# Two convolution tiles as matmuls over four taps on shifted copies, in the mixers of a two-block model

## The chip, the core and the metric

One core of a Trainium2 chip runs the whole program. Its engines work in parallel, each through its own list of instructions in order: TensorE (PE; matmuls, with weight loads as PEld), VectorE (DVE), ScalarE (ACT), GpSimd (POOL) and SyncE (SP), which here only issues transfers (DMA). Engines wait for each other by semaphores. The metric is the device time of one execution in microseconds; lower is better.

## What is computed

Batch 1, 256 positions, width 1024, float32. A first block of two layers (a gated memory cell beside retention) is followed by a second block of two layers; each of these is a mixer and a feed-forward part, dense in the first layer and a mixture of experts in the second. The change is in the mixer:

```python
def conformer_conv(u, conv_w, conv_b, ln_g, ln_b):
    a, g = jnp.split(u, 2, axis=-1)
    z = a * jax.nn.sigmoid(g)
    z = lax.conv_general_dilated(z, conv_w, window_strides=(1,),
        padding=[(CONV_WIDTH - 1, 0)], feature_group_count=D_CONV, ...) + conv_b
    z = layernorm(z, ln_g, ln_b)
    return jax.nn.silu(z)

# in each layer of the second block
proj = h @ w_in[l]
y_conv = conformer_conv(u_conv, ...)
y_att = chunk_band_attention(q, k, v, ...)      # 8 heads of 64
x = x + g1 * (jnp.concatenate([y_conv, y_att], axis=-1) @ w_out[l])
```

The convolution is depthwise and causal: 512 channels, 31 taps each, and its layer norm runs over the 512 channels.

## The kernel before

Everything lies transposed, channels on the 128 partitions and the 256 positions along the rows, so 512 channels are four tiles of 128 x 256.

**Units.** All weights go by in units of 1 MB (128 x 2048). For each unit SP loads it into a slot of `raw` (`load`), ScalarE rounds it to the matmul's type (`high`, line 730, `whi`), VectorE computes the remainder (`low`, line 1757, `wlo`), and TensorE makes three products for each tile pair (high by high, high by low, low by high). `whi` and `wlo` have three slots each: `high` of unit n waits until TensorE is done with unit n - 3 (`unit_done`). `low` hands the raw slot back to SP (`raw_free`). This order is written out by hand in each engine's part; there is no scheduler.

**A mixer** has 10 units of `w_in` (`MIX_COLS` gives the 256-column group of each) and 4 units of `w_out`. Of the 10 units two give the gate (`MIX_SIG`), two the value that it is multiplied with (`MIX_Z`), two the attention's values (`MIX_V`), and four q and k (`MIX_QK`). The functions are `mixer` in the parts of ScalarE, TensorE and VectorE, and `mixer_loads` in SP's.

- ScalarE computes the gate (`sigmoid`), takes q, k and values out of PSUM, the softmax's exponentials (`weights`, `scaled`), the turned weights (`take_turned`), and at the end squares, root and silu of the convolution's norm.
- VectorE computes z = (1 + gate) x value for two tiles at a time into `zpad`, which has 30 zeros ahead of the 256 positions. Then it goes through the taps of tiles 0 and 1, one instruction of 128 x 256 for each tap and tile (62), and after them those of tile 2 (31, in two sums, and an addition: lines 2135 and 2139). The taps are spread between the lows and the attention's steps (`conv(n)`).
- Tile 3 is TensorE's: `diag` holds for each tap a 32 x 32 diagonal of weights in each of the four groups of 32 partitions, and `conv` (line 1478) multiplies it with a shifted view of `zpad`. That is 31 taps x 4 groups = 124 products of 32 x 32 x 256, in three blocks between the attention's last steps. ScalarE takes the result (line 1019).
- `diagonals()` on VectorE builds `diag` once a mixer, with one product of 992 elements (line 2157).
- After the last attention step TensorE runs output unit 0 (`out_unit(0)`: attention's tiles, ready first), the mean over the four convolution tiles (line 1548), three adaptation rows (`ada_rows`, line 1469, products of 128 x 32 x 256 over four groups of columns), the variance (line 1555, over the squares that ScalarE made, line 1024), and output units 1 to 3.

ScalarE's order at this end matters below:

```python
act.wait_ge(tile_done, l + 1)
nc.scalar.activation(zacc[:, CT - 1], ps2[bank_g][:, 0], ACT.Identity, bias=...)
high(Unit(first + 13))
for p in range(2):
    act.wait_ge(zc_ready, 2 * l + p + 1)
    nc.scalar.activation(sq2[:, 0, 2 * p:2 * p + 2], zacc[:, 2 * p:2 * p + 2], ACT.Square)
```

`high` of unit first + 13 waits for unit first + 10, which is output unit 0.

Of the kernel before, what the change touches and what calls it, by code (L numbers as in the profile page):

```python
# [5 lines left out]
F32 = mybir.dt.float32  # L6
# [6 lines left out]
P = 128  # L13
S = 256
# [71 lines left out]
CONV_STEPS = 3 * CW + 1  # L86
# [173 lines left out]
def two_block_model(nc, x, positions, consts, c, w_ada, b_ada, norm_g, w_in, conv_w, conv_b, b_igate, b_fgate,  # L260
# [7 lines left out]
    with ctx:  # L268
# [3 lines left out]
        def sem(name):  # L272
# [95 lines left out]
        zpad = sb("zpad", [P, CT, CW - 1 + S], F32, b2)  # L368
# [14 lines left out]
        b2.close()  # L383

# [46 lines left out]
        diag = cst[:, C_CAUSAL:C_CAUSAL + CW * GROUP].rearrange("p (a m) -> p a m", a=CW)  # L431
# [51 lines left out]
        diag_ready, tile_done, tile_taken = sem("diag_ready"), sem("tile_done"), sem("tile_taken")  # L483
# [11 lines left out]
        logits_done, e_ready, route_ready, rank_done, jobs_ready, htok_done, htok_ready = (  # L495
            sem("logits_done"), sem("e_ready"), sem("route_ready"), sem("rank_done"), sem("jobs_ready"),
# [14 lines left out]
        def _(sp):  # L511
# [54 lines left out]

            def mixer_loads(l, first):
# [155 lines left out]
        def _(act):  # L723
# [186 lines left out]
            def mixer(l, first):  # L910
# [82 lines left out]
                take_values(1)  # L993
# [6 lines left out]
                sigmoid(1)  # L1000
# [18 lines left out]
                nc.scalar.activation(zacc[:, CT - 1], ps2[bank_g][:, 0], ACT.Identity, bias=par2[:, l, P2_CB + CT - 1:P2_CB + CT])\  # L1019
                    .then_inc(tile_taken, 1)  # L1020
# [45 lines left out]
            act.wait_ge(e_ready, 1)  # L1066
# [61 lines left out]
        def _(pe):  # L1128
# [289 lines left out]
            def mixer(l, first):  # L1418
# [55 lines left out]
                def conv(of):  # L1474

                    for tap in of:
                        for g in range(0, P, GROUP):
                            last = mm(ps2[bank_g][g:g + GROUP, 0], diag[g:g + GROUP, tap], zpad[g:g + GROUP, CT - 1, tap:tap + S],  # L1478
                                      start=tap == 0, stop=tap == CW - 1)
                    if of[-1] == CW - 1:  # L1480
                        last.then_inc(tile_done, 1)
# [5 lines left out]
                if l:  # L1487
# [3 lines left out]
                        8: (qk_taken, 4 * l + 4), 9: (v2_ready, 2 * l + 2)}  # L1491
# [1047 lines left out]
```

## Time and profile before

| | |
|---|---|
| three timed runs | 2111.48, 2113.81, 2115.74 us, median 2113.81 |
| profiled execution, first to last instruction (span) | 2109.6 us |
| TensorE busy | 2063.4 us (98% of the span) |
| VectorE busy | 1759.2 us (83%) |
| ScalarE busy | 1321.1 us (63%) |
| TensorE's granted clock | 0.993 of full speed over the span, 1.00 in both mixers |
| first mixer | about 643 to 762 us of the span |
| second mixer | about 972 to 1090 us |

The profiled execution has no time of its own beside its span; what lies around the span is in the timed runs only. TensorE's busy time comes from matmuls whose ends are modelled, and they overlap in the pipeline, so the idle time between them is the better sign. A printed wait in a timeline stands in brackets behind the row, with what ended it.

### The profile page before, as it was taken

Reading aid. Unit: us, or ns where it says so; the run is one execution under the profiler, and the core shown is the slowest. Engines: PE = TensorE matmul, PEld = TensorE weight load, DVE = VectorE, ACT = ScalarE, POOL = GpSimd, SP = SyncE. Lnnn points to the kernel's source line nnn. Section 1 sums busy time; section 2 is a strip of 40 time slices with the busy share of each in tenths; the row PEclk is TensorE's granted clock in tenths of the full one; section 3 lists DMA queues with packets and bytes.
Section 4 is the critical chain, followed back from the end, with each engine's and each line's share of the span. In section 5 each row is a group of like instructions: output and inputs, shape, how many; then the busy total and the mean of one; then the engine's idle time right before and its main releaser. Section 6 shows DMA issues by size and latency. Waiting matters only on the chain.

```text
span 2109.6 us, 33770 instructions
## 1 busy us (share of the span) xinstructions
PE 2063.4 (98%) x13553; PEld 1837.5 (87%) x13553; DVE 1759.2 (83%) x2177; ACT 1321.1 (63%) x1265; POOL 30.5 (1%) x60
## 2 busy tenths in 40 slices
PE   7999999999999999999989999999999999999998
PEld 5999999999999889999878888888888888888887
DVE  3898976888759888888878888888888888888887
ACT  3655645566645663435757777776777776776775
POOL 3000000000000000000000000000000000000000
PEclk8999999999999999999999999999999999999999
DMA  9788855776656379986448999999999999999995
GB/s 297 248 261 249 250 199 160 220 220 204 216 184 220 117 225 308 317 308 220 141 163 306 361 355 348 379 348 347 357 356 376 349 345 356 365 365 344 360 344 195
DMA packets 356160, 595.05 MB, mean 282 GB/s; under 512 B 10376, under 2 KB 201368, under 8 KB 356008
## 3 DMA queue, kind: packets, MB, share of 16 engines
q1 hardware_dynamic: 352864, 586.92, 80.7%
q0 software_dynamic: 2752, 5.86, 1.1%
q8 instruction: 109, 1.79, 0.4%
q14 instruction: 43, 0.35, 0.0%
q10 hardware_dynamic: 392, 0.13, 0.0%
HBM read 591.80 MB, written 4.22 MB: 283 GB/s over the span
## 4 chain that ended last, share of the span: by engine, by line
PE 84%; DVE 9%; ACT 3%; issue 2%; DMA 1%; POOL 0%; SPq 0%; DVEq 0%; POOLq 0%
PE ps L1660 9%; PE ps L1662 9%; PE ps L1661 9%; PE ps L1150 6%; PE ps L1152 5%; PE ps L1151 5%; PE ps L1691 5%; PE ps L1690 5%; PE ps L1689 5%; PE ps L1205 3%; PE ps L1207 3%; PE ps L1206 3%; DVE wlo L1757 3%; PE ps L1635 1%; PE ps L1478 1%
## 5 line engine op out<-in xcount | busy, mean ns | idle before, releaser
L1757 DVE TENSOR_TENSOR wlo<-raw,whi 128x2048 fp32r<-128x2048 f32 x485 | 1108.9, 2288 | 206.9 <-ACT whi L730 206.5
L730 ACT CAST whi<-raw 128x2048 fp32r<-128x2048 f32 x485 | 926.6, 1911 | 376.2 <-PE ps L1662 133.2
L1150 PE MATMUL ps<-hhi,whi 128*128 128x256 f32 x1360 | 387.4, 285 | 0.5 <-DVE wlo L1757 0.5
L1152 PE MATMUL ps<-hhi,wlo 128*128 128x256 f32 x1360 | 379.8, 279 | 0.0
L1151 PE MATMUL ps<-hlo,whi 128*128 128x256 f32 x1360 | 379.5, 279 | 0.0
L1660 PE MATMUL ps<-whi,xghi 128*128 128x512 f32 x896 | 360.3, 402 | 0.7 <-DVE wlo L1757 0.7
L1662 PE MATMUL ps<-wlo,xghi 128*128 128x512 f32 x896 | 350.2, 391 | 0.0
L1661 PE MATMUL ps<-whi,xglo 128*128 128x512 f32 x896 | 348.9, 389 | 0.0
L1150 PEld LDWEIGHTS ps<-hhi,whi 128*128 128x128 f32 x1360 | 255.8, 188 | 7.6 <-issue 7.3
L1151 PEld LDWEIGHTS ps<-hlo,whi 128*128 128x128 f32 x1360 | 255.9, 188 | 0.3
L1152 PEld LDWEIGHTS ps<-hhi,wlo 128*128 128x128 f32 x1360 | 255.6, 188 | 0.0
L1662 PEld LDWEIGHTS ps<-wlo,xghi 128*128 128x128 f32 x896 | 168.1, 188 | 36.6
L1660 PEld LDWEIGHTS ps<-whi,xghi 128*128 128x128 f32 x896 | 168.3, 188 | 33.9 <-DVE wlo L1757 1.2
L1661 PEld LDWEIGHTS ps<-whi,xglo 128*128 128x128 f32 x896 | 168.6, 188 | 33.6
L1689 PE MATMUL ps<-whi,thi 128*128 128x512 f32 x448 | 175.2, 391 | 0.0
L1691 PE MATMUL ps<-wlo,thi 128*128 128x512 f32 x448 | 174.8, 390 | 0.0
L1690 PE MATMUL ps<-whi,tlo 128*128 128x512 f32 x448 | 174.6, 390 | 0.0
L1813 DVE SCALAR_TENSOR_TENSOR acc<-raw,cact,acc 128x256 f32<-128x256 f32 x324 | 132.8, 478 | 0.0
L1691 PEld LDWEIGHTS ps<-wlo,thi 128*128 128x128 f32 x448 | 84.1, 188 | 17.8
L1690 PEld LDWEIGHTS ps<-whi,tlo 128*128 128x128 f32 x448 | 84.1, 188 | 16.9
L1689 PEld LDWEIGHTS ps<-whi,thi 128*128 128x128 f32 x448 | 84.1, 188 | 16.8
L1191 PE MATMUL ps<-whi,hhi 128*128 128x256 f32 x320 | 91.8, 287 | 0.0
(400 smaller groups left out, 2991.4 us busy)
## 6 DMA issues: line engine op xcount, KB each, us to landing
raw<-in_moe_w_gate_dram SPq DMA_DIRECT2D x112, 1024.0 KB, 5.9
raw<-in_moe_w_up_dram SPq DMA_DIRECT2D x112, 1024.0 KB, 5.8
raw<-in_moe_w_down_dram SPq DMA_DIRECT2D x112, 1024.0 KB, 5.2
raw<-in_w_in_dram SPq DMA_DIRECT2D x92, 1024.0 KB, 5.5
raw<-in_w_ada_dram SPq DMA_DIRECT2D x69, 1024.0 KB, 7.9
raw<-in_w_out_dram SPq DMA_DIRECT2D x24, 1024.0 KB, 5.2
raw<-in_ffn_w_gate_dram SPq DMA_DIRECT2D x11, 1024.0 KB, 9.2
raw<-in_ffn_w_up_dram SPq DMA_DIRECT2D x11, 1024.0 KB, 9.1
```

Source lines behind the costliest of these rows:

```text
L730: nc.scalar.copy(whi[:, u.hl, :], raw[:, u.raw, :]).then_inc(hi_ready, 1)
L1150: mm(ps2[u.bank][:, j], whi[:, u.hl, w], hhi[:, k], start=k == 0, stop=False)
L1151: mm(ps2[u.bank][:, j], whi[:, u.hl, w], hlo[:, k], start=False, stop=False)
L1152: last = mm(ps2[u.bank][:, j], wlo[:, u.hl, w], hhi[:, k], start=False, stop=k == KD - 1)
L1660: mm(o, xghi[:, k, x], whi[:, u.hl, w], start=k == 0, stop=False)
L1661: mm(o, xglo[:, k, x], whi[:, u.hl, w], start=False, stop=False)
L1662: last = mm(o, xghi[:, k, x], wlo[:, u.hl, w], start=False, stop=k == KD - 1)
L1689: mm(o, thi[:, f], whi[:, u.hl, w], start=f == 0, stop=False)
L1690: mm(o, tlo[:, f], whi[:, u.hl, w], start=False, stop=False)
L1691: last = mm(o, thi[:, f], wlo[:, u.hl, w], start=False, stop=f == FE // P - 1)
L1757: V.tensor_tensor(wlo[:, u.hl, :], raw[:, u.raw, :], whi[:, u.hl, :].bitcast(F32), ALU.subtract).then_inc(raw_free, 1)
L1813: last = V.scalar_tensor_tensor(sums[k % 2], w[:, k], cact[:, block, k:k + 1], sums[k % 2], ALU.mult, ALU.add)
```

## The change

In each of the two mixers:

- Tiles 2 and 3 are both TensorE's. For each tile t and each group g of 32 channels, SP makes four copies of the group's rows of `zpad`, each one position further on, and stacks them on the 128 partitions. A product with such a stack (128 rows) and a matrix of 128 x 32 that holds four diagonals sums four taps. 31 taps are 8 steps (`TAP_STEPS`), each reading the stack four positions further. 2 tiles x 8 steps x 4 groups = 64 products of 128 x 32 x 256.
- The copies are `shifts(l)`, 20 transfers from SP: 12 of 32 x 2 x 284 elements (both tiles) and 8 of 32 x 284. They go into `h`, which is free then, and the last stack into `acc`. SP issues them behind the load of unit first + 12 and waits for z of tiles 2 and 3 first. Loads of later units stand behind them.
- VectorE's `diagonals()` builds two matrices of 128 x 1024 in place of one of 128 x 992, from 16 small copies of taps. They lie in the parts of `y2hi` and `y2lo` that are written later. VectorE keeps the taps of tiles 0 and 1 only.
- The gate's second unit comes one place forward (units 7 and 8 give z of tiles 2 and 3, unit 9 the second half of the values), `z(1)` stands right behind the low part of unit 9, `sigmoid(1)` takes the place of `take_values(1)` on ScalarE, and that stands later.
- On TensorE adaptation rows and mean stand ahead of output unit 0; the variance stands behind it.
- In the expert layer the semaphore `e_ready` is merged into `route_ready`.

The diff, cut to its core:

```diff
-MIX_COLS = (2, 0, 4, 6, 8, 5, 7, 9, 3, 1)
-MIX_SIG, MIX_Z, MIX_V, MIX_QK = (0, 8), (1, 9), (4, 7), (2, 3, 5, 6)
+MIX_COLS = (2, 0, 4, 6, 8, 5, 7, 3, 1, 9)
+MIX_SIG, MIX_Z, MIX_V, MIX_QK = (0, 7), (1, 8), (4, 9), (2, 3, 5, 6)
...
+            def shifts(l):
+                sp.wait_ge(z_ready, 2 * l + 2)
+                for g in range(P // GROUP):
+                    for o in range(TAPS_AT_ONCE):
+                        to, of = slice(GROUP * o, GROUP * o + GROUP), zpad[GROUP * g:GROUP * g + GROUP, 2:4, o:o + ZW]
+                        if g < 3:
+                            sp.dma_start(zflat[to, 2 * ZW * g:2 * ZW * g + 2 * ZW].rearrange("p (t x) -> p t x", t=2), of).then_inc(shifted_in, 16)
+                        else:
+                            for t in range(2):
+                                sp.dma_start(shifted(t, g)[to], of[:, t]).then_inc(shifted_in, 16)
...
                     load(Unit(first + MIX_UNITS + j), ...)
+                    if j == 2:
+                        shifts(l)
...
# ScalarE
-                take_values(1)
+                sigmoid(1)
                 pair_high(0)
...
-                sigmoid(1)
                 pair_high(1)
...
                     take_turned(n)
+                take_values(1)
                 for n in (6, 7):
                     weights(n)
...
-                act.wait_ge(tile_done, l + 1)
-                nc.scalar.activation(zacc[:, CT - 1], ps2[bank_g][:, 0], ...)
+                for t in range(2):
+                    act.wait_ge(tile_done, 2 * l + t + 1)
+                    nc.scalar.activation(zacc[:, 2 + t], ps2[bank_g][:, t], ...)
                 high(Unit(first + 13))
...
# TensorE
+                def conv(t, of):
+                    for m in of:
+                        for g in range(P // GROUP):
+                            at = GROUP * (TAP_STEPS * g + m)
+                            last = mm(ps2[bank_g][GROUP * g:GROUP * g + GROUP, t], sdiag[t][:, at:at + GROUP],
+                                      shifted(t, g)[:, TAPS_AT_ONCE * m:TAPS_AT_ONCE * m + S], start=m == 0, stop=m == TAP_STEPS - 1)
...
-                pe.wait_ge(sig_ready, 2 * l + 2)
                 pe.wait_ge(z_ready, 2 * l + 2)
-                conv(range(0, 10))
+                pe.wait_ge(shifted_in, 16 * SHIFTS * (l + 1))
+                conv(0, range(TAP_STEPS))
+                pe.wait_ge(v2_ready, 2 * l + 2)
                 weighted(4)
                 weighted(5)
-                conv(range(10, 18))
+                conv(1, range(4))
                 turn_weights(6)
                 turn_weights(7)
-                conv(range(18, CW))
+                conv(1, range(4, TAP_STEPS))
                 weighted(6)
                 weighted(7)
-                out_unit(0)
+                for i in range(rows - HALF, rows):
+                    ada_rows(i)
+                pe.wait_ge(conv_step, CONV_STEPS * (l + 1))
                 for t in range(CT):
...
                     last = mm(ps2[bank_a][:, 0], mean512[:], zacc[:, t], start=t == 0, stop=t == CT - 1)
                 last.then_inc(zmean_done, 1)
-                for i in range(rows - HALF, rows):
-                    ada_rows(i)
+                out_unit(0)
...
# VectorE
-                    V.tensor_tensor(diag, sel.unsqueeze(1).broadcast_to([P, CW, GROUP]), ...)
+                    of = taps2[:, l].rearrange("p (m o t) -> p o t m", o=TAPS_AT_ONCE, t=CT)
+                    for o in range(TAPS_AT_ONCE):
+                        for g in range(P // GROUP):
+                            last = V.tensor_copy(wst[GROUP * o:GROUP * o + GROUP, :, g], of[GROUP * g:GROUP * g + GROUP, o, 2:4])
+                    step(last)
+                    for t in range(2):
+                        last = V.tensor_tensor(sdiag[t][:]..., sel..., wst[:, t]..., ALU.mult)
...
                 low(Unit(first + 9))
+                z(1)
...
                 low(Unit(first + 10))
-                z(1)
...
-                conv(4)
+                conv(len(taps))
                 pair_low(2)
-                conv(len(taps) - 8)
                 pair_low(3)
-                conv(len(taps))
                 dve.wait_ge(zmean_done, l + 1)
```

How instructions stand on the engines, at three places of the first mixer.

TensorE, its end, before: the last products of output unit 0 (line 1205 and on), mean (`mean512` with `zacc`), adaptation rows (`cpad`), variance (`mean512` with `h`), and output unit 1.

```order
L1205 MATMUL ps5<-y2hi,whi 128x256
L1206 MATMUL ps5<-y2lo,whi 128x256
L1207 MATMUL ps5<-y2hi,wlo 128x256
L1548 MATMUL ps1<-zacc,mean512 128x256 x4
L1469 MATMUL ps7<-raw,cpad 32x256 x24
L1555 MATMUL ps0<-h,mean512 128x256 x4
L1205 MATMUL ps2<-y2hi,whi 128x256
```

The same end now, from the last weighted sums (`pT,v2`) to the start of output unit 0:

```order
L1488 MATMUL ps6<-pT,v2 64x256
L1489 MATMUL ps6<-pT,v2 64x128
L1499 MATMUL ps7<-raw,cpad 32x256 x24
L1580 MATMUL ps1<-zacc,mean512 128x256 x4
L1235 MATMUL ps2<-y2hi,whi 128x256
```

and from the end of output unit 0 on:

```order
L1235 MATMUL ps5<-y2hi,whi 128x256
L1236 MATMUL ps5<-y2lo,whi 128x256
L1237 MATMUL ps5<-y2hi,wlo 128x256
L1586 MATMUL ps0<-h,mean512 128x256 x4
L1235 MATMUL ps2<-y2hi,whi 128x256
```

Mean and adaptation rows went ahead of output unit 0, and nothing stands between it and the variance any more. On ScalarE the order there is the one before: take the tiles, high part of unit 13, squares.

SP, its transfers at the end of the first mixer, before: the four loads of output units stand in a row, behind the last ones of `w_in`.

```order
L520 DMA raw<-in_w_in_2_dram 128x8x256
L533 DMA raw<-in_w_ada_2_dram 128x8x256
L520 DMA raw<-in_w_out_2_dram 128x2x1024 x4
L520 DMA raw<-in_ffn_w_gate_2_dram 128x8x256
L533 DMA raw<-in_w_ada_2_dram 128x8x256
```

Now:

```order
L535 DMA raw<-in_w_out_2_dram 128x2x1024 x3
L589 DMA h<-zpad 32x2x284 x12
L592 DMA h<-zpad 32x284
L592 DMA acc<-zpad 32x284
L592 DMA h<-zpad 32x284
L592 DMA acc<-zpad 32x284
L592 DMA h<-zpad 32x284
L592 DMA acc<-zpad 32x284
L592 DMA h<-zpad 32x284
L592 DMA acc<-zpad 32x284
L535 DMA raw<-in_w_out_2_dram 128x2x1024
```

The 20 copies stand ahead of the load of the last output unit.

VectorE, the preparation of the diagonals behind the first z, before:

```order
L2117 SCALAR_TENSOR_TENSOR zpad<-sig,ps1 128x2x256
L2151 MEMSET cst 64x64
L2152 MEMSET cst 64x64
L2155 MEMSET cst 64x64 x2
L2156 TENSOR_REDUCE cst<-cst 128x32
L2157 TENSOR_TENSOR cst<-cst,taps2 128x992
L1757 TENSOR_TENSOR wlo<-raw,whi 128x2048
```

Now:

```order
L2149 SCALAR_TENSOR_TENSOR zpad<-sig,ps1 128x2x256
L2178 MEMSET cst 64x64
L2179 MEMSET cst 64x64
L2182 MEMSET cst 64x64 x2
L2183 TENSOR_REDUCE cst<-cst 128x32
L2187 COPY cst<-taps2 32x2x8 x16
L2190 TENSOR_TENSOR sdiag0<-cst 128x1024
L2190 TENSOR_TENSOR sdiag1<-cst 128x1024
L1788 TENSOR_TENSOR wlo<-raw,whi 128x2048
```

The low part of unit 4 stands behind 16 copies and two products where it stood behind one product.

## Rows read from the trace of the kernel before

**Rows 1.** Table of stretches, first mixer: busy us (instructions) by engine, clock, DMA share, GB/s
```profile
core 0: us, PE busy (x) PEld busy (x) DVE busy (x) ACT busy (x) POOL busy (x), PEclk, DMA share, GB/s
640.00:770.00 130.00, 125.65 (x1190) 110.36 (x1189) 109.13 (x226) 83.53 (x140) 0.91 (x1) 1.00 0.55 179
```

**Rows 2.** Timeline of TensorE, first mixer: start us, length us, engine, line, operation, count
```profile
715.46 4.52 PE L1478 MATMUL ps<-zpad,cst 32*32 32x256 f32 x80 [0.36 <-DVE zpad L2117]
...
720.72 3.66 PE L1478 MATMUL ps<-zpad,cst 32*32 32x256 f32 x64
...
725.12 5.82 PE L1478 MATMUL ps<-zpad,cst 32*32 32x256 f32 x104
...
731.67 0.39 PE L1205 MATMUL ps<-y2hi,whi 128*128 128x256 f32 x1
...
737.52 1.89 PE L1548 MATMUL ps<-zacc,mean 128*128 128x256 f32 x8
739.34 2.80 PE L1469 MATMUL ps<-raw,cpad 128*32 128x256 f32 x48
742.07 1.99 PE L1555 MATMUL ps<-h,mean 128*128 128x256 f32 x8
```

**Rows 3.** Timelines of VectorE (first row) and ScalarE, end of the first mixer
```profile
735.85 0.42 DVE L2139 TENSOR_TENSOR zacc<-zacc,sig 128x256 f32<-128x256 f32 x1
...
737.78 1.90 ACT L730 CAST whi<-raw 128x2048 fp32r<-128x2048 f32 x1 [5.21 <-PE ps L1207]
740.17 1.23 ACT L1024 ACTIVATE h<-zacc 128x512 f32<-128x512 f32 x2 [0.49 <-DVE zacc L2253]
```

**Rows 4.** Timeline of VectorE, first mixer: low part of unit 9, second z
```profile
705.30 2.28 DVE L1757 TENSOR_TENSOR wlo<-raw,whi 128x2048 fp32r<-128x2048 f32 x1
...
714.63 0.68 DVE L2117 SCALAR_TENSOR_TENSOR zpad<-sig,ps 128x512 f32<-128x512 f32 x1
```

**Rows 5.** Transfers: issues by SP and ScalarE (timelines), median us to landing, landings in mixer
```profile
0.72 0.77 SPq L513 DMA_DIRECT2D crow<-in_c_dram  x2
1.54 0.36 SPq L514 DMA_DIRECT2D cst<-in_consts_dram  x1
...
1.40 0.28 ACTq L788 DMA_DIRECT2D prow<-in_norm_g_dram  x1
...
2103.01 1.84 SPq L620 DMA_DIRECT2D out_dram<-h  x4
...
707.62 0.37 SPq L520 DMA_DIRECT2D raw<-in_w_out_dram  x1
...
out_dram<-h SPq DMA_DIRECT2D x4, 256.0 KB, 2.9
...
cst<-in_consts_dram SPq DMA_DIRECT2D x1, 64.0 KB, 1.9
...
DMA to landing us min/median/max: 4.8/8.0/13.3
```

**Rows 6.** Timelines of VectorE and TensorE, first mixer: diagonals, small operations, heads, scores
```profile
661.30 1.19 DVE L2157 TENSOR_TENSOR cst<-cst,taps 128x992 f32<-128x992 f32 x1
...
754.78 0.23 DVE L2271 TENSOR_TENSOR mod<-ps,par 128x6 f32<-128x6 f32 x2
...
651.78 0.18 DVE L2190 COPY cpad<-cact 128x8 f32<-128x8 f32 x1
...
680.62 1.41 DVE L2146 SCALAR_TENSOR_TENSOR q<-q,par,rs 128x512 f32<-128x512 f32 x2
...
682.11 0.50 PE L1440 MATMUL ps<-q 64*128 64x128 f32 x4
```

**Rows 7.** Timelines of VectorE and TensorE, second mixer: waits, heads, scores
```profile
994.68 2.29 DVE L1757 TENSOR_TENSOR wlo<-raw,whi 128x2048 fp32r<-128x2048 f32 x1 [0.60 <-ACT whi L730]
...
1007.20 0.75 DVE L2146 SCALAR_TENSOR_TENSOR q<-q,par,rs 128x512 f32<-128x512 f32 x1 [0.37 <-ACT rs L942]
...
1009.34 0.50 PE L1440 MATMUL ps<-q 64*128 64x128 f32 x4
...
1016.56 1.24 PE L1449 MATMUL ps<-cst,p 128*128 128x128 f32 x6 [0.50 <-ACT p L957]
```

More of the change, by code:

```diff
@@ L367, in two_block_model @@
         y2lo = sb("y2lo", [P, KD, S], F32R, b2)
-        zpad = sb("zpad", [P, CT, CW - 1 + S], F32, b2)
+        zpad = sb("zpad", [P, CT, CW + S], F32, b2)
         zacc = sb("zacc", [P, CT, S], F32, b2)
@@ L383, in two_block_model, with shifted @@
         b2.close()
+        bd = ExitStack()
+        sdiag = [sb("sdiag0", [P, TAP_STEPS * P], F32, bd)]
+        sb("between_sdiag", [P, (KD - CT) * S], F32, bd)
+        sdiag.append(sb("sdiag1", [P, TAP_STEPS * P], F32, bd))
+        bd.close()
+        zflat = h[:].rearrange("p k s -> p (k s)")
+        zspare = acc[:, 0:2].rearrange("p k s -> p (k s)")
+        def shifted(t, g):
+            return zspare[:, 0:ZW] if (t, g) == (1, P // GROUP - 1) else zflat[:, ZW * (2 * g + t):ZW * (2 * g + t) + ZW]
         bf = ExitStack()
@@ L1472, in ada_rows @@
                     last.then_inc(ada_done, 1)
[L1474 to L1480, printed above, removed]
+                def conv(t, of):
[4 more added lines that the diff above has]
+                                      shifted(t, g)[:, TAPS_AT_ONCE * m:TAPS_AT_ONCE * m + S], start=m == 0, stop=m == TAP_STEPS - 1)
+                    if of[-1] == TAP_STEPS - 1:
                         last.then_inc(tile_done, 1)
@@ L2108, in mixer @@
                 n0, bank_a = NH2 * l, Unit(first + 9).bank
-                taps = [(t, tap) for tap in range(CW) for t in range(2)] + [(2, tap) for tap in range(CW)]
+                taps = [(t, tap) for tap in range(CW) for t in range(2)]
                 done = CONV_STEPS * l
@@ L2116, in z @@
                     dve.wait_ge(unit_done, u.done())
-                    V.scalar_tensor_tensor(zpad[:, 2 * i:2 * i + 2, CW - 1:], sig[:], 1.0, ps2[u.bank], ALU.add, ALU.mult)\
+                    V.scalar_tensor_tensor(zpad[:, 2 * i:2 * i + 2, CW - 1:CW - 1 + S], sig[:], 1.0, ps2[u.bank], ALU.add, ALU.mult)\
                         .then_inc(z_ready, 1)
@@ L2124, in conv @@
                         t, tap = taps.pop(0)
-                        at = done + 3 * CW - len(taps)
-                        to = sig[:, 1] if t == 2 and tap % 2 else zacc[:, t]
+                        at = done + CONV_STEPS - len(taps)
+                        to = zacc[:, t]
                         w, src = taps2[:, l, tap * CT + t:tap * CT + t + 1], zpad[:, t, tap:tap + S]
@@ L2130, in conv @@
                             last = V.tensor_scalar(to, src, w, par2[:, l, P2_CB + t:P2_CB + t + 1], ALU.mult, ALU.add)
-                        elif t == 2 and tap == 1:
-                            last = V.tensor_scalar(to, src, w, None, ALU.mult)
                         else:
@@ L2136, in conv @@
                         last.then_inc(conv_step, 1)
-                        if not taps:
-                            dve.wait_ge(conv_step, at)
-                            V.tensor_tensor(zacc[:, 2], zacc[:, 2], sig[:, 1], ALU.add).then_inc(conv_step, 1)
                 def norm_heads(half):
@@ L2186, in mixer @@
                 V.memset(zpad[:, :, 0:CW - 1], 0.0)
+                V.memset(zpad[:, :, CW - 1 + S:], 0.0)
                 V.memset(mean512[:], 1.0 / D_CONV)
```

39 lines of the change are left out of this document (22 added, 17 removed).

## The prediction

> **What bounds the kernel now.** I read the table of stretches first: in the first mixer's stretch TensorE is busy 125.65 of 130 us, VectorE 109.13 [rows 1]. So TensorE is the engine to shorten, and a microsecond counts where TensorE works less or waits less. Next the timeline of the first mixer's second half [rows 2]. The reader is to see a TensorE that hardly stops: the three convolution blocks start at 715.46, 720.72 and 725.12, output unit 0 at 731.67, the mean at 737.52, the adaptation rows at 739.34, the variance at 742.07, each about where the one before it ends. The only printed wait is 0.36 before the convolution. The second mixer runs the same code. Busy times of adjacent groups overlap by some hundredths, so sums below are good to about 0.1 a term.
>
> **Convolution on TensorE.** Now 124 products of form 32x32 take 4.52 + 3.66 + 5.82 = 14.00 us [rows 2]. (The counts there are twice as large, since weight loads are counted too.) Afterwards there are 2 tiles x 8 steps x 4 groups = 64 products of form 128x32. That form is in the trace: 24 adaptation products, also over four column groups, take 2.80, 0.117 each [rows 2]. 64 x 0.117 = 7.5. **-6.5 per mixer.** I see no reason for much less or more: same form, same columns, same type.
>
> **VectorE loses its third tile**, 31 taps and an addition. That work is not on the path: its last addition runs from 735.85 to 736.27 [rows 3], and the mean follows output unit 0 at 737.52 [rows 2] without a wait. Removed it gives **0** by itself; it only lets the mean stand ahead of output unit 0.
>
> **The shifted copies, a new wait.** The convolution now needs 20 transfers, which SP issues after z of the second pair. z moves right behind the low part of unit 9, which ends at 705.30 + 2.28 = 707.58, and takes 0.68 [rows 4]: done at 708.2. SP issued the load that stands ahead, unit 12's, at 707.62 for 0.37 [rows 5], so it is free. What do 20 issues cost? Two issues at the program's start span 0.72 to 1.54, 0.41 each [rows 5]. The twentieth starts at 708.2 + 19 x 0.41 = 716.0. How long a small transfer takes from issue to landing has two near rows: 1.9 (64 KB into SBUF) and 2.9 (256 KB to DRAM) [rows 5]. A copy has 71 KB, so I take 2.0: all landed at 718.0. The convolution started at 715.46. **+2.5 per mixer**, the printed wait of 0.36 included. Behind this wait on TensorE stand weighted sums 4 to 7 and everything after them; nothing can step in. Bounds: the quickest issue of a small load is 0.28 [rows 5], 0.31 apart, and 1.9 to land gives 716.0 (+0.5); four stores in 1.84, 0.46 apart [rows 5], and 2.9 to land give 719.8 (+4.3).
> SP's next load, unit 13's, slips by two microseconds from 714.7 and is not needed before output unit 0 is over. ScalarE's second sigmoid changes places with taking the values; its table load falls into ScalarE's wait for unit 7, and what is left (some tenths later for weights 4 and 5) lies under the wait for the copies.
>
> **Squares behind a cast, a second new wait.** On ScalarE the order at the end is unchanged: take the tiles, high part of unit 13, squares. The high part waits until output unit 0 is done: it ran at 737.78, 0.26 after the mean's start, for 1.90, and the squares followed at 740.17 [rows 3]. Today TensorE has the mean (1.89) and the adaptation rows (2.80) in that time and arrives at the variance at 742.07 [rows 2], after the squares. In the change the mean and the rows stand ahead of output unit 0, and the variance directly behind it. So after output unit 0 TensorE waits for 0.26 + 1.90 and the first square, half of 1.23: 0.26 + 1.90 + 0.62 = 2.8. **+2.75 per mixer**; I see no smaller end than 2.4, as ScalarE's order is fixed, and none above 3.2. What follows the variance (root, scaling, silu) follows it as before, under output unit 1.
>
> **VectorE's preparation.** It gets 16 copies of 16 elements and two products of 1024 elements in place of one of 992. Two small operations take 0.23 together, 0.15 for the second and so 0.08 from start to start [rows 6]: 15 x 0.08 + 0.15 = 1.4. The product of 992 takes 1.19 [rows 6], one of 1024 so 1.23, and 1.2 is added. Sum +2.6. If each copy costs what the 128x8 copy takes alone, 0.18 [rows 6], it is 2.9 + 1.2 = +4.1; I take the nearer row, two in succession.
> Who pays? In the first mixer's timeline VectorE has no wait from 661.30 until it has normalized the heads, 680.62 to 682.03, and TensorE's first scores stand at 682.11 [rows 6], 0.08 later. (Lows and taps fill the time between.) So the delay reaches TensorE: **+2.5 in the first mixer**. In the second, VectorE waits 0.60 and then 0.37, its normalized heads are ready at 1007.95 for scores at 1009.34, 1.4 later, and TensorE waits 0.50 at 1016.56 for ScalarE [rows 7]. Together 2.9. That takes up the delay: **+0.1 in the second**.
> The Trainium skill speaks against many small operations here. Its page VectorE: DVE Perf Modes, section The TRN2 errata, gives a fixed cost for each instruction, 58 cycles by its table and about 150 by its measurement of single operations, at 0.96 GHz. By 150 the 16 copies would take an estimated 2.8 us instead of 1.4, and the sum would be 1.4 higher; by 58 they take 1.2, which agrees with the row of two in succession, 0.08 apart.
>
> **The sum.** First mixer: -6.5 + 2.5 + 2.75 + 2.5 = +1.25. Second: -6.5 + 2.5 + 2.75 + 0.1 = -1.15. Together +0.1. The profiled execution has a span of 2109.6; the median of the runs, 2113.81, lies 4.2 above it, and I add the same: 2109.7 + 4.2 = 2113.9. A measurement of this kernel can tell about 0.2%, 4.2 us, from no change: the bounds are 2109.6 and 2118.0.
>
> **Rivals.**
> Slower: the copies queue behind the load issued 0.6 earlier. Loads of a megabyte in this stretch, some of them issued right behind another, took 4.8 to 13.3 to land [rows 5]; the 20 copies are another megabyte behind unit 12's. Should they be done 13.3 after 708.2, at 721.5, each mixer loses 3.5 more: 2113.9 + 7.0 = 2120.9. It turns out slower by over 0.2% once the copies land more than 2.1 later than 718.0 in both mixers. For it: each copy touches 32 partitions at a time, which no row shows. Against it: the transfer engines are busy 0.55 of this stretch [rows 1], and 20 issues spread the copies over 8 us. Costly copies on VectorE (+1.5, first mixer) push the same way.
> By the Trainium skill, page SBUF — State Buffer, section Door 1, a transfer over 32 partitions reaches 8 of 16 ports, 27.2 GB/s each. By that a copy's 73 KB need an estimated 0.33 us, less than an issue; only together with the load ahead would it end past the last issue, by some tenths. No row here has such a transfer.
> Faster: issue and landing go at their quick ends, 2.0 less per mixer, 2109.9; if VectorE's delay in the first mixer is taken up as well (2.5), 2107.4. Against the latter speaks the 0.08 above.
> The change doesn't do what it says: the 128x32 products do not overlap over column groups. A full product takes 1.89 / 4 = 0.47 [rows 2]; 64 of them cost 30 instead of 7.5, +45 for both mixers, 2159. The adaptation rows at 0.117 speak against it.
>
> **How the numbers follow.** Forecast 0.62; slower rival with costly copies 0.24; faster rival 0.13; no overlap 0.01. The forecast and the quick end at 2109.9 lie within 0.2%, but part of the faster rival's chance lies past 2109.6. Faster 0.12, same 0.63, slower 0.25. The bounds of the issues (-4.0, +3.6) and of the copies (+1.5) span 2109.9 to 2119.0; with a part of both rivals the range is 2108 to 2120.
>
> **What would show it.** In the trace of the changed kernel: 64 convolution products in 7.5 us a mixer; TensorE waiting some 2.5 (2 to 3) for a transfer of zpad before the first of them; a second wait of 2.75 before the variance, behind ScalarE's cast; a stall of 2.5 spread over unit 4 and the first scores in the first mixer only; the third tile's taps gone from VectorE without effect. The prediction is wrong if the copies land before TensorE gets there, if the squares are ready at the end of output unit 0, or if unit 4 and the scores start on time.

## The result, and the profile after

The changed kernel takes 2132.86 us (median of 4 runs, 2132.27 to 2133.36); the kernel before took 2114.05 in the same rounds. The ratio is 1.009, with a 95% interval of 1.0078 to 1.0103: **slower by 18.8 us**. The forecast was 2113.9 with a range up to 2120. It was wrong. Its chance for this side, 0.25, stood mainly on copies that queue behind a load, which did not happen, and for a small part on costly copies on VectorE, which did. The profiled executions have spans of 2109.6 before and 2131.5 after, 21.9 apart; the accounts below are made against these 21.9. The profiled execution after is that of the slowest run (2133.36), 0.5 above the median. Besides, a run's time exceeds its span by 1.9 in the changed kernel and by 2.3 to 3.0 in the kernel before, in the rounds of the experiments; the forecast had added 4.2. The rest of the 3.1 us by which 21.9 exceeds 18.8 is less than the spread of the kernel before, 4.3.

Lines of the changed kernel lie 27 to 35 further down: the convolution is L1509, the variance L1586, the output units L1235 to L1237, the cast L759, the low part L1788, the copies' issues L589 and L592.

First the page of the kernel after: TensorE is at 97% of a longer span.

```profile
span 2131.5 us, 33306 instructions
...
PE 2062.4 (97%) x13313; PEld 1836.9 (86%) x13313; DVE 1741.7 (82%) x2151; ACT 1321.8 (62%) x1267; POOL 30.6 (1%) x60
```

Next the waits of TensorE: us in total, times, longest. Before, the convolution waited twice for z (0.36 in the first mixer [rows 2]), 0.7 in all, and no counterpart of the other three was over 0.5.

```profile
PE ps L1509 <- DMA acc<-zpad: 14.6, 2, 7.4
...
PE ps L1586 <- ACT h L1054: 5.1, 2, 2.6
...
PE ps L1221 <- DVE wlo L1788: 3.2, 3, 2.7
...
PE ps L1470 <- DVE q L2173: 1.3, 1, 1.3
```

The first is the wait for the copies, twice 7.3. The second is the wait for the squares, twice 2.57. The last two stand behind the preparation on VectorE: unit 4 in the first mixer (2.7) and the first scores in the second (1.3). Together 24 us, where the forecast had 5.0 + 5.5 + 2.6 = 13.

Then the timeline of TensorE. The first three rows are the first mixer, the last two the second mixer's first scores and convolution; in brackets the wait just before.

```profile
668.65 0.36 PE L1221 MATMUL ps<-whi,hhi 128*128 128x256 f32 x1 [2.73 <-DVE wlo L1788]
...
726.63 5.78 PE L1509 MATMUL ps<-h,sdiag 128*32 128x256 f32 x64 [7.11 <-DMA acc<-zpad]
...
751.54 3.62 PE L1586 MATMUL ps<-h,mean 128*128 128x256 f32 x8 [2.57 <-ACT h L1054]
...
1023.12 0.50 PE L1470 MATMUL ps<-q 64*128 64x128 f32 x4 [1.30 <-DVE q L2173]
...
1064.26 5.93 PE L1509 MATMUL ps<-h,sdiag 128*32 128x256 f32 x64 [7.45 <-DMA acc<-zpad]
```

Two things are to be seen. The waits for the copies are near 7, not 2.5. And what comes right behind a wait is slow: the variance's products take 3.62, where before they took 1.99 [rows 2]; the first 32 convolution products (counted as 64 with their loads) take 5.78, where 3.66 is their time at full speed, as an experiment below shows; and some 16 products of unit 4 start 0.21 apart where 0.12 is usual, 1.6 us in all. The table of stretches says why (busy us by engine, TensorE's clock as a share of full speed, share of the transfer engines, GB/s):

```profile
core 0: us, PE busy (x) PEld busy (x) DVE busy (x) ACT busy (x) POOL busy (x), PEclk, DMA share, GB/s
668.70:672.70 4.00, 4.00 (x22) 4.00 (x23) 4.00 (x12) 0.29 (x1) 0.00 (x0) 0.60 0.76 251
...
719.00:726.00 7.00, 0.53 (x6) 0.12 (x3) 6.04 (x20) 4.02 (x14) 0.00 (x0) 0.87 0.33 79
726.00:733.00 7.00, 6.37 (x72) 3.48 (x72) 0.00 (x0) 0.00 (x0) 0.00 (x0) 0.64 0.45 155
733.00:740.00 7.00, 7.00 (x111) 3.96 (x110) 0.85 (x2) 4.15 (x7) 0.00 (x0) 1.00 0.00 0
...
751.50:754.50 3.00, 2.96 (x7) 2.43 (x8) 0.00 (x0) 2.04 (x3) 0.00 (x0) 0.50 1.03 325
...
778.00:781.00 3.00, 3.00 (x19) 3.00 (x19) 3.00 (x9) 3.00 (x8) 0.00 (x0) 0.63 0.01 3
...
1064.00:1068.00 4.00, 3.75 (x36) 2.02 (x40) 0.00 (x0) 0.00 (x0) 0.00 (x0) 0.50 0.76 266
```

While TensorE waits, or within a microsecond of its new start (unit 4), its clock falls from 2.4 to 1.2 GHz (a share of 0.50), and it stays there for some microseconds of work. Before, the first mixer stood at 1.00 throughout [rows 1]. The page TensorE: Matmul & The Clock Gate of the Trainium skill, section HAM oscillation — how this bites in real kernels, describes this: a wait for a transfer between blocks of products puts the clock down, and the block behind the wait starts at the low level. The trace agrees, and the prediction had no term for it. Not every wait has this behind it: the start of the dense layer waits 2.17 in both kernels, and the products behind it ran at 1.00 before and at 0.63 after (778 to 781). Which short waits put the clock down stays open.

SP's timeline tells where the 7 us come from (SPq is SP issuing a transfer).

```profile
711.94 8.16 SPq L589 DMA_DIRECT2D h<-zpad  x12
720.15 0.59 SPq L592 DMA_DIRECT2D h<-zpad  x1
...
724.64 0.59 SPq L592 DMA_DIRECT2D acc<-zpad  x1
```

Twenty issues take 13.3 us, from 711.94 to 725.23. Transfers of zpad land 1.9 to 5.3 after their issue, 2.2 in the median; TensorE starts at 726.63, 2.0 after the last issue began. So the last copy arrives as fast as forecast, but the copies are sent 0.63 to 0.68 apart instead of 0.41.

VectorE's preparation, and ScalarE at the end of the first mixer:

```profile
661.04 2.87 DVE L2187 COPY cst<-taps 32x16 f32<-32x16 f32 x16
663.94 2.36 DVE L2190 TENSOR_TENSOR sdiag<-cst 128x1024 f32<-128x1024 f32 x2
```

```profile
749.06 1.90 ACT L759 CAST whi<-raw 128x2048 fp32r<-128x2048 f32 x1 [9.29 <-PE ps L1237]
750.86 1.14 ACT L1054 ACTIVATE h<-zacc 128x512 f32<-128x512 f32 x2
```

**Account of the 21.9 us.** The changed kernel comes to the first mixer 0.3 earlier than the kernel before. In the first mixer: unit 4 and what follows it +4.1, for VectorE is that late (it begins to normalize the heads at 684.43, before at 680.62 [rows 6], and the 0.3 comes on top); TensorE spends it as a wait of 2.73 and as low clock behind it. Weights 4 and 5 +0.6, since ScalarE does its second sigmoid ahead of them; the wait for the copies +6.75 (7.11 less the 0.36 of before); the convolution -6.5 in products, +2.1 for the low clock; the wait for the squares +2.57, and +1.6 for the variance at the low clock. Sum +11.2; the timelines say that the mixer takes 11.4 longer. Second mixer: +1.0 preparation (the wait of 1.30, less some tenths taken back behind it), +0.6, +7.1 (7.45 less the 0.31 of before), -6.5 + 2.3, +2.57, +1.6, sum +8.7; the timelines say +8.9. The start of the dense layer behind the first mixer costs 1.2 more, by the clock of 0.63 shown above; the start of the expert layer behind the second costs 0.5 more, by a wait of 3.64 instead of 3.15. 11.4 + 8.9 + 1.2 + 0.5 - 0.3 = 21.7. These are readings; the experiments test the parts.

### The profile page after: what moved, and what is told of

Its sections match the earlier page's. It is cut to its first block, busy times and chain, and to the rows that moved or that the text cites. A ratio compares the mean times of both kernels' runs of the same rounds, so it can differ in the third digit from the quotient of the medians.

```text
span 2131.5 us, 33306 instructions
## 1 busy us (share of the span) xinstructions
PE 2062.4 (97%) x13313; PEld 1836.9 (86%) x13313; DVE 1741.7 (82%) x2151; ACT 1321.8 (62%) x1267; POOL 30.6 (1%) x60
## 4 chain that ended last, share of the span: by engine, by line
PE 82%; DVE 9%; ACT 3%; issue 3%; DMA 2%; SPq 1%; DVEq 0%; ACTq 0%
PE ps L1693 9%; PE ps L1691 9%; PE ps L1692 9%; PE ps L1180 5%; PE ps L1181 5%; PE ps L1182 5%; PE ps L1722 5%; PE ps L1721 5%; PE ps L1720 5%; PE ps L1235 3%; PE ps L1236 3%; PE ps L1237 3%; DVE wlo L1788 3%; PE ps L1666 1%; ACT whi L759 1%
## 5 line engine op out<-in xcount | busy, mean ns | idle before, releaser
L1788 DVE TENSOR_TENSOR wlo<-raw,whi 128x2048 fp32r<-128x2048 f32 x485 | 1108.8, 2288 | 205.7 <-ACT whi L759 205.3
L759 ACT CAST whi<-raw 128x2048 fp32r<-128x2048 f32 x485 | 926.6, 1911 | 384.1 <-PE ps L1693 133.6
```

The lines of the kernel that those rows point to most:

```text
L759: nc.scalar.copy(whi[:, u.hl, :], raw[:, u.raw, :]).then_inc(hi_ready, 1)
L1788: V.tensor_tensor(wlo[:, u.hl, :], raw[:, u.raw, :], whi[:, u.hl, :].bitcast(F32), ALU.subtract).then_inc(raw_free, 1)
```

## Experiments

The theory after the result (A in the expectations): the loss has four parts, the copies' issues on SP, the clock that falls in the waits, the preparation on VectorE, and the squares behind the cast. The main rivals: the transfers themselves are slow or disturb other traffic, and the issue is dearer because of where its data comes from.

Times "below the change" are differences of medians from different rounds; in them the kernel before had 2114.05 (the change), 2113.81 (experiments 1 to 4) and 2112.84 (6 and 7). With the intervals of the ratios a difference of 5 can be 2 or 8, so where two accounts lie closer the rows decide and not the time.

**1. The copies left out.** The change without its 20 transfers and without the wait for them; its convolution of tiles 2 and 3 reads whatever lies in the buffers, so it is a measurement and not a kernel to use.

```diff
-                    if j == 2:
-                        shifts(l)
...
-                pe.wait_ge(shifted_in, 16 * SHIFTS * (l + 1))
```

> The changed kernel without its 20 copies a mixer and without TensorE's wait for them (part left out: the convolution of tiles 2 and 3 reads whatever lies in the buffers). Theory A (the loss is mostly the wait for the copies, 7.1 and 7.45 us, and the clock that it halves, 5.78 instead of 3.64 us for the first 32 products, twice): 14.6 + 4.3 = 18.9 us less than the changed kernel, 2114. Rival B (the 128x32 products are slow by themselves after the attention's products): the wait goes but the first block stays at 5.8 us, 2118. Rival C (the wait only takes the place of another, on ScalarE or VectorE): above 2124.

Measured: 2112.7 us, ratio 0.9995 (0.9985 to 1.0004). The copies and what hangs on them cost 20.2 us: 14.6 of waiting, 4.4 of low clock in the convolution by the timelines, and 1.2 that this run does not assign. Its first 32 products run at full clock:

```profile
719.76 3.66 PE L1507 MATMUL ps<-h,sdiag 128*32 128x256 f32 x64
```

What follows is sobering: even if the copies were free, the change would only break even. It saves 13 us of products, and the two other waits, with their clock, take these back.

**2. Squares ahead of the cast.** One line of ScalarE's order moved.

```diff
-                high(Unit(first + 13))
                 for p in range(2):
                     act.wait_ge(zc_ready, 2 * l + p + 1)
                     nc.scalar.activation(sq2[:, 0, 2 * p:2 * p + 2], zacc[:, 2 * p:2 * p + 2], ACT.Square).then_inc(zsq_ready, 1)
+                high(Unit(first + 13))
```

> The changed kernel with ScalarE's two squares ahead of the high part of unit 13. Theory A (TensorE's 2.57 us before the variance is ScalarE's order, and the variance's slow 3.6 instead of 2.0 us is the clock that this wait halves): 2 x (2.57 + 1.6) = 8.3 us less, 2124.5. Rival B (the clock is halved by the earlier, longer wait anyway): 5.1 us less, 2127.7. Rival C (something else, such as VectorE's subtraction, is late by as much): under 2 us less.

Measured: 2124.85, ratio 1.0055 (1.0038 to 1.0072), 8.0 below the change, as expected. By the time alone that is not clear of the 5.1 of the two waits; the row is, for the variance is back at full clock and directly behind output unit 0. (A new wait of 0.9 a mixer, for VectorE's low part ahead of output unit 1, takes a part back.)

```profile
748.52 1.89 PE L1586 MATMUL ps<-h,mean 128*128 128x256 f32 x8
```

**3. TensorE kept busy while it waits.** 58 products whose results are not used stand ahead of the wait for the copies; the copies are untouched.

```diff
+                for _ in range(58):
+                    mm(ps2[bank_g][:, 0], hhi[:, 0, 0:P], hhi[:, 0], start=True, stop=True)
                 pe.wait_ge(shifted_in, 16 * SHIFTS * (l + 1))
```

> The changed kernel with 58 products without use (128x256, 0.117 us each, 6.8 us) between the last scores and the wait for the copies; nothing waits for them. Theory A (the first block takes 5.8 us because the granted clock is halved after 7 us without work): the clock stays at 1.00, the block takes 3.7, 2 x 2.1 = 4.2 us less than the changed kernel, 2128.7. Rival B (the block's length is the products' own, or bank or operand effects): no gain, and if the products overrun the wait, a loss of up to 1 us.

Measured: 2128.37, ratio 1.0065 (1.0048 to 1.0082), 4.5 below the change. The convolution starts as long behind the first copy's issue as in the change (14.7), and its first 32 products take 3.66 instead of 5.78, in the second mixer too:

```profile
726.06 3.66 PE L1509 MATMUL ps<-h,sdiag 128*32 128x256 f32 x64
```

So the second part of the loss at the copies is the clock, not the form of the products.

**4. The copies in the kernel before, with nobody on TensorE waiting.** In the first mixer they come from zpad, in the second the same shapes come from a weight in DRAM.

```diff
+                        to, of = slice(GROUP * o, GROUP * o + GROUP), zpad[GROUP * g:GROUP * g + GROUP, 2:4, o:o + 283]
+                        if l:
+                            of = w_in_2[1].rearrange("(k p) n -> p k n", p=P)[GROUP * g:GROUP * g + GROUP, 2:4, o:o + 283]
...
+                    if j == 2:
+                        shifts(l)
```

> The kernel before with 20 such copies a mixer added behind the load of unit 12; in the first mixer from zpad, in the second of the same shape from a weight in DRAM. TensorE waits for none (the squares at the end do, long after). Theory A (an issue of such a copy holds SP for 0.59 us and more wherever it comes from, since 20 stand in a row; the copies themselves disturb nobody): issues 0.63 apart in both mixers, time within 0.1% of the kernel before. Rival B (the source in SBUF makes the issue dear): 0.63 in the first mixer, 0.41 in the second. Rival C (traffic of the copies slows loads): over 2 us slower than before.

Measured: 2114.17, ratio 1.0001 (0.9991 to 1.0011). The traffic costs nothing that shows (the interval is 2 us either way), so it is the waiting for it that costs. SP's timeline, first mixer and then the second:

```profile
715.32 8.31 SPq L577 DMA_DIRECT2D h<-zpad  x12
723.68 0.59 SPq L579 DMA_DIRECT2D h<-zpad  x1
...
1044.46 6.73 SPq L577 DMA_DIRECT2D h<-in_w_in_dram  x12
1051.23 0.42 SPq L579 DMA_DIRECT2D h<-in_w_in_dram  x1
1051.70 0.42 SPq L580 DMA_DIRECT2D acc<-in_w_in_dram  x1
```

The same shape costs SP 0.59 from zpad and 0.42 from DRAM. The rows by line add that the first twelve are no dearer each; a few long ones lift their mean (ns, shortest / median / longest):

```profile
L577 SPq DMA_DIRECT2D h<-zpad x12: 594/597/1120, 715.3 to 723.0; - x12
L577 SPq DMA_DIRECT2D h<-in_w_in_dram x12: 343/427/1647, 1044.5 to 1050.8; - x12
```

**5. Source, place, rows or bytes?** Two looks, both again with transfers that no product waits for. First, from zpad, 20 transfers of one row of 100 numbers, over 32 partitions in the first mixer and over 128 in the second:

```diff
+                for i in range(20):
+                    if l:
+                        sp.dma_start(zflat[:, 100 * i:100 * i + 100], zpad[:, 2 + i % 2, i // 2:i // 2 + 100]).then_inc(shifted_in, 16)
+                    else:
+                        part = slice(GROUP * (i % 4), GROUP * (i % 4) + GROUP)
+                        sp.dma_start(zflat[part, 100 * i:100 * i + 100], zpad[0:GROUP, 2 + i % 2, i // 2:i // 2 + 100]).then_inc(shifted_in, 16)
```

> The kernel before with 20 transfers from zpad in SBUF issued by SP where the change issues its copies; nobody on TensorE waits for them. First mixer: 20 transfers of 32 partitions with one row of 100 numbers (12.5 KB); second mixer: 20 transfers of 128 partitions with one row of 100 numbers (50 KB). Theory A (the source decides what an issue costs): both series are 0.6 to 0.65 us apart, as the transfers of zpad of 32 partitions with 283 numbers were (0.635), whatever the bytes. Rival B (the number of rows decides, for a given source): the series of 128 partitions is clearly dearer, at or above the 0.69 of the transfers with 64 rows, and the series of 32 partitions stays at 0.635. Rival C (the bytes decide): the series of 12.5 KB falls below 0.5. The time stays within 0.2% of the kernel before in each case.

Second, from DRAM, the change's shapes in the first mixer and 128 partitions in the second:

```diff
+                        to, of = slice(GROUP * o, GROUP * o + GROUP), rows_in[GROUP * g:GROUP * g + GROUP, 2:4, o:o + 283]
...
+                        sp.dma_start(zflat[:, 100 * i:100 * i + 100], rows_in[:, 2 + i % 2, i // 2:i // 2 + 100]).then_inc(shifted_in, 16)
```

> The kernel before with 20 transfers from DRAM issued by SP where the change issues its copies; nobody on TensorE waits for them. First mixer: the 20 transfers in the shape of the change (32 partitions, two rows of 283 numbers, the last eight with one row), from a weight in DRAM. Second mixer: 20 transfers of 128 partitions with one row of 100 numbers from the same weight. It answers whether the cheaper issue from DRAM came from the source or from the place: that run had SBUF as the source in the first mixer and DRAM in the second. Theory A (the source): the first mixer's last eight are 0.47 apart, as they were in the second. Rival D (the place): they are 0.635 apart. For the series of 128 partitions theory A expects about 0.47, rival B (rows decide) 0.56 or more. The time stays within 0.2% of the kernel before in each case.

One time each, 2114.7 and 2113.53 beside 2112.41 of the kernel before. SP's rows by line, of the run from zpad (32 partitions, then 128):

```profile
L576 SPq DMA_DIRECT2D h<-zpad x20: 577/591/1484, 714.7 to 728.5; - x20
...
L573 SPq DMA_DIRECT2D h<-zpad x20: 533/602/1823, 1044.1 to 1057.9; - x20
```

and of the run from DRAM (the change's shapes, then 128 partitions):

```profile
L578 SPq DMA_DIRECT2D h<-in_w_in_dram x12: 348/427/1602, 714.8 to 721.1; - x12
...
L584 SPq DMA_DIRECT2D h<-in_w_in_dram x20: 340/432/1212, 1043.7 to 1053.4; - x20
```

The median is 0.59 to 0.60 from zpad and 0.42 to 0.43 from DRAM, whatever the place, the partitions (32 or 128) or the bytes (12.5 to 71 KB). Theory A, the source, holds for the median; rivals B, C and D fall. The means came out dearer than I expected, though: 0.73 apart from zpad instead of 0.60 to 0.65, and 0.51 instead of 0.47 from DRAM, by single issues of 1.2 to 1.8 us. What makes those is open. So is whether the source alone decides: the four stores from h to DRAM, also from SBUF, are 0.46 apart [rows 5].

**6. The preparation moved.** The 16 copies and two products no longer stand with the diagonals but some steps later, behind conv(4) and conv(6), where VectorE has slack.

```diff
                 conv(4)
+                prep_copies()
                 pair_low(0)
                 conv(6)
+                prep_products()
                 norm_heads(1)
```

> The changed kernel with VectorE's 16 small copies and two products moved from ahead of unit 4's low part to places where VectorE waits later (copies ahead of the low part of heads 0 and 1, products ahead of the second normalization of heads). Theory A (their 5.2 us instead of 1.2 reach TensorE through unit 4 and the first scores, 4.1 in the first mixer and 1.0 in the second, and cost a half clock after the 2.7 us wait): 5 us less than the changed kernel, 2128. Rival (VectorE is that full everywhere, the delay comes back at unit 9 or the copies): under 2 us less.

Measured: 2127.84, ratio 1.0067 (1.0053 to 1.0082), 5.0 below the change, or 3.8 if each is set against the kernel before of its own rounds. The wait of unit 4 is gone from the first mixer and that of the first scores from the second; the wait for the copies is a little longer:

```profile
PE ps L1509 <- DMA acc<-zpad: 15.2, 2, 7.8
```

**7. All of it together, and who issues.** The edit is cut to its main lines. Squares first; preparation moved; the adaptation rows placed ahead of the wait for the copies, as 2.8 us of work that covers it; 16 copies instead of 20 (the fourth stack goes to a free part of the constants' tile and needs no second piece); ScalarE takes the tiles a step earlier, and VectorE's step conv(3) goes to the taps that it does last. In this version SP issues all 16:

```diff
-SHIFTS = 4 * 5
+SHIFTS = 4 * 4
...
-        zspare = acc[:, 0:2].rearrange("p k s -> p (k s)")
+        zspare = cst[:, C_CAUSAL + 64:C_CAUSAL + 64 + 2 * ZW]
...
+                for i in range(rows - HALF, rows):
+                    ada_rows(i)
                 pe.wait_ge(diag_ready, l + 1)
```

> The changed kernel with all that the runs point to: squares ahead of the high part of unit 13, preparation moved, the adaptation rows ahead of the wait for the copies, 16 copies of both tiles instead of 20 (the fourth stack in the free part of the diagonals' old place), three taps moved behind the biases of heads 4 and 5. All copies from SP. Theory: 16 issues 0.68 apart from z on and 2.1 to land come 12.3 us behind z; TensorE with the adaptation rows is there 2 us earlier and waits that. Each mixer then gains 6.5 + 0.4 for the convolution and loses 2 for the wait, 0.3 for the preparation, 0.9 for the last low part and up to 1.6 for the clock: 2 to 3.3 less than before, 2107.5 to 2110. Rival (the wait is longer since copies of both tiles need more than an issue each, or the order has another wait): 2112 or more.

Measured: 2109.1, ratio 0.998 (0.9971 to 0.9988). Then SP issues 11, and the last five of the 16 go to GpSimd, whose queue is empty there:

```diff
+                pool.wait_ge(z_ready, 2 * l + 2)
+                shift(pool, range(11, 16), bias_in)
```

> As the one before, but the last 5 of the 16 copies are issued by GpSimd, which is idle there. Theory: SP's last of 11 issues stands 6.9 us behind z and lands 2 later, 9 behind z, which TensorE meets 10.3 behind z without a wait, if GpSimd's five take no more than 10 (its transfers of 24 to 192 KB took 5 to land). Then each mixer gains 5.4 against before, 2103.5. Rival (GpSimd's issues take over 1 us each, or VectorE's operations hold them up): the wait stays at 2 or grows, 2108 or more.

Measured: 2104.99, ratio 0.9958 (0.9946 to 0.9971). And, in place of that, SP issues 12 and the last four go to ScalarE:

```diff
                 high(Unit(first + 11))
+                act.wait_ge(z_ready, 2 * l + 2)
+                shift(act, range(12, 16), shifted_in)
                 for n in (4, 5):
```

> As e7_all_sp, but the last 4 of the 16 copies are issued by ScalarE between the high part of unit 11 and the weights of head 4. Theory: SP's 12 issues land 10 behind z, without a wait for TensorE; ScalarE's 4 issues take 2.5 us and delay the weights of heads 4 and 5 by 1.4, which TensorE waits for. Each mixer gains 4 against before, 2106. Rival (ScalarE's queue shares the descriptor generation with SP's, so issues slow each other): as e7_all_sp or slower.

Measured: **2102.62**, ratio 0.9948 (0.9936 to 0.996), 10.2 us below the kernel before in the same rounds, where the change as made lay 18.8 above it in its own. I had expected 2106, for fear that the copies would hold up ScalarE's exponentials or that two queues would slow each other. The wait for the copies in the three versions, one row from each in that order:

```profile
PE ps L1513 <- DMA cst<-zpad: 6.5, 2, 3.3
```

```profile
PE ps L1515 <- DMA h<-zpad: 3.0, 2, 1.8
```

```profile
PE ps L1515 <- DMA h<-zpad: 1.7, 2, 0.8
```

The three differ in little but who issues the last few copies. From the first to the second the wait falls from 6.5 to 3.0 and the time from 2109.1 to 2105.0, with no run of the one in the range of the other: the length of the one queue of issues did set the wait. The step from GpSimd to ScalarE proves nothing more. The intervals overlap, the profiled spans are 2102.7 and 2102.3, and the shorter wait is only TensorE's later coming. TensorE's timeline of the second mixer, first with GpSimd, then with ScalarE (unit 11, weights of head 4 where they are waited for, convolution):

```profile
1030.39 0.36 PE L1227 MATMUL ps<-whi,hhi 128*128 128x256 f32 x1 [0.20 <-DVE wlo L1795]
...
1042.34 0.42 PE L1515 MATMUL ps<-h,sdiag 128*32 128x256 f32 x3 [1.78 <-DMA h<-zpad]
```

```profile
1032.74 0.36 PE L1227 MATMUL ps<-whi,hhi 128*128 128x256 f32 x1 [0.20 <-DVE wlo L1794]
...
1039.05 1.24 PE L1485 MATMUL ps<-cst,p 128*128 128x128 f32 x6 [0.40 <-ACT p L986]
...
1044.68 0.42 PE L1515 MATMUL ps<-h,sdiag 128*32 128x256 f32 x3 [0.81 <-DMA h<-zpad]
```

The convolution starts 11.95 and 11.94 behind unit 11, against 13.36 when SP issues all. So ScalarE's exponentials were held up, as feared, and it shows in front of the wait, as 0.5 in the first mixer and 1.0 in the second; the wait covers it. Nor are the transfers without a part: with all 16 from SP their median from issue to landing was 2.6, with GpSimd 4.9 and with ScalarE 4.8. The split saves issue time and gives some of it back in landing.

The issues of the last version, SP's and then ScalarE's, start at the same time:

```profile
707.84 8.82 SPq L529 DMA_DIRECT2D h<-zpad  x12
```

```profile
707.84 2.67 ACTq L529 DMA_DIRECT2D cst<-zpad  x4
```

And the clock stays up in the stretch that stood at 0.64 after the change:

```profile
726.00:733.00 7.00, 7.00 (x70) 5.56 (x71) 2.80 (x4) 3.00 (x7) 0.00 (x0) 1.00 0.01 2
```

## Why the prediction was wrong, point by point

- **Convolution on TensorE, -6.5 a mixer: right in the products, not in what arrived.** 32 of them take 3.66 at full clock, so 64 take 7.3 to 7.5 as forecast. In the change the first half ran at the low clock, +2.1 and +2.3, so the block brought -4.3.
- **Shifted copies, +2.5 a mixer: the term that failed most.** The step "0.41 each" was mis-sized: it came from two loads from DRAM at the program's start, and the copies go from SBUF to SBUF at 0.63 to 0.68. Over 19 gaps that is 4.2 to 5.1 us. The landing, 2.0, was right, and so was the place of the first issue, 0.6 behind the load ahead of it. My upper bound, 0.46 apart from four stores and 2.9 to land, was below the truth too: the bound was made from rows of the wrong kind, and nothing in the text said that none of them was a transfer within SBUF. The printed waits came out at 7.11 and 7.45. Measured as the term was meant, from where TensorE would have come without the sigmoid's delay below, the copies cost 7.4 and 7.7 a mixer, not 2.5.
- **The clock: no term at all.** The prediction named a wait of 2.5 and one of 2.75 on an engine whose clock stood at 1.00, and let the work behind them go on at full speed. 2.1 + 2.3 behind the copies and 1.6 + 1.6 behind the squares make 7.6 us. Experiments 2 and 3 show it by their rows, 1.89 instead of 3.62 and 3.66 instead of 5.78, and their times agree: 8.0, where the squares' waits alone are 5.1, and 4.5, where nothing but the clock was changed. The wait of 2.57 for the squares already had the low clock behind it. The 1.2 at the start of the dense layer looks the same, but no run takes it apart. The low clock behind unit 4's wait, 1.6, is not added: VectorE's heads were late by nearly as much as wait and clock together, and the first scores need them.
- **Squares behind the cast, +2.75 a mixer: right**, 2.57 twice, with the order and the place as written. Only the clock behind it was missing.
- **Preparation, +2.6 and of it 2.5 on the path: mis-sized.** The 16 copies take 2.87, 0.18 each, and the products 1.18 each, sum 5.2 less the 1.2 of before: +4.1. That was the upper end, what the 128x8 copy takes alone. I took 0.08 from a pair of another operation, which reads PSUM, where the copies go from SBUF to SBUF, and so gave the wrong one of two rows the weight. The Trainium skill's page VectorE: DVE Perf Modes, section The TRN2 errata, had both figures; the measured fixed cost of about 150 cycles gives 2.8 us by estimate, and the trace agrees with 2.87. The second mixer paid +1.0, not +0.1, by the same error: its slack was about the 2.9 that I had read, and 4.1 less 2.9 is 1.2. The two together, 5.1, agree with the 3.8 to 5.0 of experiment 6.
- **The second sigmoid: "some tenths later" and covered: right.** It came to 0.6 a mixer, and it does lie under the wait: SP starts the copies as soon as z is done (711.92 and 711.94), the convolution starts 14.7 behind that, and TensorE's coming 0.6 later to the wait only shortens what is printed of it. In the account above 0.6 and 6.75 are therefore one cost. No run takes the sigmoid alone.
- **VectorE's third tile, 0: right by what was seen**; no wait on its additions appears after.
- **The rivals.** The slower one had the sign but not the reason: copies queueing behind unit 12's load, landing 13.3 after issue. They land in 2.2 in the median, and experiment 4 shows the traffic to be harmless. The price it gave, 2120.9, was 12 us short. Its other half, costly copies on VectorE at +1.5 in the first mixer, did come true. The faster one and the one without overlap fell.

By the forecast's own sum with the measured terms: first mixer -6.5 + 7.4 + 2.57 + 4.1 = +7.6, second -6.5 + 7.7 + 2.57 + 1.0 = +4.8, together 12.4, or 2126. The issues (10 us more than forecast) and the preparation (2.5) thus explain about two thirds of the miss of 19, and the clock with its 7.6 the rest.

## What to carry to other kernels

Count the issues of a transfer that is cut into pieces, and price each from a row with the same two ends (SBUF to SBUF here 0.6 us, not the 0.4 of a load); where many pieces are awaited, split them over queues of engines that have time. A wait of 2.6 us and more that a change puts on a TensorE at full clock needs a second term, for the products behind it at half speed (the waits of 0.8 to 1.8 in the last two versions had none behind them), and that is a reason to look for independent work to put ahead of the wait. A change that takes work off the busiest engine can still lose it all to the order of the engines that feed it: two moved lines on ScalarE and VectorE were worth about 8 and 4 to 5 us here, nearly the whole saving of 13.

## What the runs showed of the hardware

- An issue on SP took 0.59 to 0.60 in the median for transfers from SBUF to SBUF and 0.42 to 0.43 from DRAM to SBUF in a row, independent of 12.5 to 71 KB and of 32 or 128 partitions; now and then one took 1.1 to 1.8. A load right behind the copies from SBUF also took 0.58, one right behind those from DRAM 0.43. ScalarE's four took 2.67, about the same each, beside SP's and without slowing them by more than 0.4 in twelve (8.82 against 8.42 when SP issues alone). The landings did get slower: 2.6 in the median with SP alone, 4.8 with ScalarE and 4.9 with GpSimd beside it.
- The clock of TensorE stood at half after waits of 7.1 and 7.45, and also behind one of 2.57; the work behind them took 1.6 to 2.3 us more than its time. Behind one of 2.73 it fell 0.8 us after the start. A wait of 2.17 had 1.00 behind it in one kernel and 0.63 in the other.
- Copies of 32x16 between partitions took 0.18 each in a row of sixteen on VectorE, as much as a single copy of 128x8 takes [rows 6]: they got no cheaper by following one another.
